# Turns three steps behind the scores, and values four, in the first sixteen steps of three attentions

## The reference

```python
for l in range(DEPTH):                      # DEPTH = 1
    h = _rmsnorm(x, norm_mix[l])
    proj = h @ w_in[l]
    (c_q, c_kv, k_rope, fq, fk, fv, f_logit, cq, ck, cv) = jnp.split(proj, IN_SPLIT_POINTS, axis=-1)
    ya = _mla(c_q, c_kv, k_rope, ...)        # latent: 4 heads, values of 128, all earlier chunks
    yb = _fox(fq, fk, fv, f_logit, ...)      # forgetting: 4 heads of 64, causal, decay in the scores
    yc = _chunk_rel(cq, ck, cv, rel_bias[l]) # chunk: 4 heads of 64, 8 chunks of 64 to the left
    y = jnp.concatenate([_rmsnorm(ya, ga), _rmsnorm(yb, gb), _rmsnorm(yc, gc)], axis=-1)
    x = x + y @ w_o[l]
```

```python
sc = jnp.einsum('bqhd,bkhd->bhqk', qb, k) * scale   # scores, plus a bias or a mask
p = jax.nn.softmax(sc, axis=-1)
out = jnp.einsum('bhqk,bkhd->bqhd', p, v)
```

## Time and profile before

| | |
|---|---|
| median of 3 runs | 2356.68 us (2355.68 to 2357.24) |
| span of the profiled execution, first to last instruction | 2354.8 us |
| PE busy | 2301.3 us (98%) |
| DVE, ACT, POOL busy | 61%, 41%, 37% |
| mean granted TensorE clock | 0.994 |

### The profile page before, as it was taken

One profiled execution on the slowest core, in us unless ns is written; L12 is line 12 of the kernel. 1 busy time (PEld: TensorE's weight loads), 2 busy tenths in 40 slices (PEclk: granted clock), 3 DMA queues, 4 the chain that ended last, 5 costly groups with the idle time before them and its releaser, 6 DMA issues. The chain is left out here.

```text
span 2354.8 us, 30600 instructions
## 1 busy us (share of the span) xinstructions
PE 2301.3 (98%) x11502; PEld 1936.4 (82%) x11502; DVE 1444.1 (61%) x2287; ACT 966.9 (41%) x1963; POOL 872.2 (37%) x737
## 2 busy tenths in 40 slices
PE   6999999999999999999999999999999999999998
PEld 5887878888888888888998887888888888888886
DVE  6999924955354577775634767253495545447776
ACT  4135544532323245455634655134453233234543
POOL 3000125388787800032112121122338878770002
PEclk9999999999999999999999999999999999999999
DMA  5131124233233368664002100144223323336864
GB/s 156 44 71 64 63 83 133 88 119 112 90 116 103 116 242 290 212 209 115 19 19 70 46 5 19 54 143 143 81 72 116 117 85 117 103 122 244 289 214 182
DMA packets 219445, 275.84 MB, mean 117 GB/s; under 512 B 17243, under 2 KB 144956, under 8 KB 216482
## 3 DMA queue, kind: packets, MB, share of 16 engines
q1 hardware_dynamic: 200594, 210.57, 28.7%
q10 hardware_dynamic: 18704, 63.32, 6.9%
HBM read 205.27 MB, written 68.57 MB: 116 GB/s over the span
## 5 line engine op out<-in xcount | busy, mean ns | idle before, releaser
L494 PE MATMUL P<-ah,wh 128*128 128x512 f32 x1120 | 439.3, 392 | 3.2 <-DVE al L524 2.3
L496 PE MATMUL P<-ah,wl 128*128 128x512 f32 x1120 | 436.7, 390 | 0.0
L495 PE MATMUL P<-al,wh 128*128 128x512 f32 x1120 | 436.6, 390 | 0.0
L494 PE MATMUL P<-wh,ah 128*128 128x512 f32 (+2 forms) x1128 | 425.4, 377 | 0.0
L496 PE MATMUL P<-wh,al 128*128 128x512 f32 (+2 forms) x1128 | 423.3, 375 | 0.0
L495 PE MATMUL P<-wl,ah 128*128 128x512 f32 (+2 forms) x1128 | 422.9, 375 | 0.0
L576 POOL TENSOR_TENSOR stats<-stats,epsc 128x1 f32<-128x1 f32 x78 | 31.9, 408 | 794.3 <-ACT xn L1824 420.9
L494 PEld LDWEIGHTS P<-ah,wh 128*128 128x128 f32 x1120 | 210.9, 188 | 47.3 <-DVE al L524 2.5
L496 PEld LDWEIGHTS P<-ah,wl 128*128 128x128 f32 x1120 | 210.8, 188 | 44.1
L495 PEld LDWEIGHTS P<-al,wh 128*128 128x128 f32 x1120 | 210.9, 188 | 43.0
L496 PEld LDWEIGHTS P<-wh,al 128*128 128x128 f32 x1128 | 212.3, 188 | 36.9
(11 more groups left out here) (357 smaller groups left out, 4295.9 us busy)
## 6 DMA issues: line engine op xcount, KB each, us to landing
rf<-ff_rows SPq DMA_DIRECT2D x154, 256.0 KB, 5.3
stage<-in_w_down_dram SPq DMA_DIRECT2D x110, 256.0 KB, 3.7
ff_rows<-sb ACTq DMA_DIRECT2D x22, 1024.0 KB, 5.0
stage<-in_w_gu_dram SPq DMA_DIRECT2D x44, 512.0 KB, 5.1
stage<-in_w_in_dram SPq DMA_DIRECT2D x22, 512.0 KB, 4.0
stage<-in_w_gate_dram SPq DMA_DIRECT2D x22, 512.0 KB, 4.0
stage<-in_w_up_dram SPq DMA_DIRECT2D x22, 512.0 KB, 5.2
ff_rows<-uo ACTq DMA_DIRECT2D x22, 512.0 KB, 3.0
```

Source lines behind the costliest of these rows:

```text
L494: e.matmul(out, lh, rh, start=start, stop=False, skip_group_check=onto)
L495: e.matmul(out, lh, rl, start=False, stop=False, skip_group_check=onto)
L496: return e.matmul(out, ll, rh, start=False, stop=stop, skip_group_check=onto)
```

## The change

In steps 0 to 15 the turns stand three iterations behind the scores and the values four (`lag` is 3 while x < `deep` = 16); from step 16 on it is two and three as before. The two rules meet in iteration 18, where the turns of steps 15 and 16 both fall, and 19, where the values of both fall. For the longer distance there is a fourth buffer of probabilities of 512 columns, in memory that is free then. What hangs on the end of a block (`o`, squares, scaled rows, its turn and its lower half) moves with the values of its last head: for blocks 0 to 3 it comes one iteration later. In forgetting attention the turns of chunk attention's blocks move from iterations 0, 3, 7, ... 27 to 0, 4, 8, ... 28. Sends and filling work keep their iterations. Cross attention keeps the old distances (`deep = 0`). No instruction is added or removed.

```diff
+        deep = 16
...
+        def lag(self, x):
+            return 3 if x < self.deep else 2
+
+        def turned_at(self, it):
+            return [x for x in (it - 3, it - 2) if 0 <= x < self.n and x + self.lag(x) == it]
+
+        def ended_at(self, it):
+            for x in self.turned_at(it - 1):
+                if self.at(x)[1] == self.nh - 1:
+                    return self.at(x)[0]
+            return None
...
+        def prob_free(self, port, x):
+            earlier = [y for y in range(x) if set(self.places(y)) & set(self.places(x))]
+            if earlier:
+                port.wait_ge(*self.last_turn(earlier[-1]))
...
         def pe(self):
-                if 2 <= it <= self.n + 1:
-                    x = it - 2
+                for x in self.turned_at(it):
...
-                if it >= 3:
-                    x = it - 3
+                for x in self.turned_at(it - 1):
...
         def act(self):
-                if 2 <= it <= self.n + 1:
-                    self.copy_turned(AC, it - 2)
+                for x in self.turned_at(it):
+                    self.copy_turned(AC, x)
...
     class Chunked(Heads):
-        probs = [big(f"s2_{i}", [128, 640], 50 + 2.5 * i) for i in range(3)]
+        probs = [big(f"s2_{i}", [128, 640], 50 + 2.5 * i) for i in range(3)] + [
+            sb("s2_3", [128, 512], off["extra"] + 12 * KB)]
...
     class Fox(Heads):
+        narrow_probs = [sb(f"p3n_{i}", [128, 512], off["ah"] + 4 * KB * i) for i in range(3)] + [big("p3n_3", [128, 512], 56)]
...
         def turn_key(self, it):
-            if it >= 9 and it % 4 == 1 and (it - 9) // 4 < NT:
-                return self, (it - 9) // 4
-            if self.kind == "fox" and (it == 0 or it > 0 and it % 4 == 3) and (it + 1) // 4 < NT:
-                return chunked, (it + 1) // 4
+            i = self.ended_at(it - 3)
+            if i is not None:
+                return self, i
+            if self.kind == "fox" and it % 4 == 0 and it // 4 < NT:
+                return chunked, it // 4
...
     class Latent(Fox):
+        narrow_probs = [sb(f"p4n_{i}", [128, 512], off["extra"] + kb * KB) for i, kb in enumerate((0, 4, 8, 2))]
...
-            if it == 3:
+            if it == 4:
                 port.wait_ge(cp, ("mv", 3))
...
     class Cross(Fox):
+        deep = 0
```

More of the change, by code:

```diff
@@ L2960, in act @@
                     W, _, src = self.view(it)
-                    dst = self.probs[it % 3][:, 0:W]
+                    dst = self.prob(it)[:, 0:W]
                     AC.wait_ge(sm, (self.kind, "nm", it))
-                    if it >= 3:
-                        AC.wait_ge(*self.last_turn(it - 3))
+                    self.prob_free(AC, it)
                     e.activation(dst, dst if self.biased else src, ACT.Exp, bias=head_cols(it)[0],
                                  accum_out=head_rows(i)[0][:, h:h + 1]).then_inc(*ex.up((self.kind, it)))
-                if it >= 3 and self.at(it - 3)[1] == self.nh - 1:
-                    self.square(self.at(it - 3)[0])
+                if self.ended_at(it) is not None:
+                    self.square(self.ended_at(it))
                 if it in self.sends:
@@ L2987, in dve @@
             for it in range(self.n + 3):
-                if 2 <= it <= self.n + 1:
-                    self.copy_turned(DV, it - 2)
+                for x in self.turned_at(it):
+                    self.copy_turned(DV, x)
                 self.turned_dve(it - 1)
@@ L3261, in later_dve @@
         def later_dve(self, it):
-            if it >= 7 and it % 4 == 3:
-                i = (it - 7) // 4
+            i = self.ended_at(it - 1)
+            if i is not None:
                 self.scaled(i, yc[:, i, :], gout[:, 768:1024])
@@ L3531, in pt, with places, prob @@
             return self.turned[x % 2][g // 4][:, g % 4:g % 4 + w, :]
+        def places(self, x):
+            return (self.narrow_places[x % 4],) if x < self.deep else ((x % 3, 0), (x % 3, 1))
+        def prob(self, x):
+            return self.narrow_probs[x % 4] if x < self.deep else self.probs[x % 3]
         def width(self, i):
@@ L3623, in later_dve @@
         def later_dve(self, it):
-            if it >= 7 and it % 4 == 3 and (it - 7) // 4 < NT:
-                i = (it - 7) // 4
+            i = self.ended_at(it - 1)
+            if i is not None:
                 self.scaled(i, self.outs[i % 2][:, :], gout[:, self.gain[0]:self.gain[1]])
```

26 lines of the change are left out of this document (15 added, 11 removed).

## The result

The changed kernel takes **2374.79 us** (median of 5 runs, 2374.26 to 2375.81) where the kernel before took 2356.68 on the same chip: a ratio of 1.0074, 95% interval 1.0064 to 1.0085. It is 18.1 us slower; I had said 5.6 us, 2362.3, with a range that ended at 2368. The direction was right, the size was not. The profiled execution spans 2372.5 us, TensorE is busy 2307.9 of them (97%).

A forecast was written before the change was run, and what follows sets the result against it. TensorE, busy 98%, bounds the kernel; only its idle time and slow stretches can change. Chunk +0.3, forgetting +2.8 and latent +2.5 sum to 5.6 us: 2362.3 us against 2356.7, range 2354 to 2368.

The forecast's parts named there:

- What bounds the kernel: Whole kernel: TensorE, busy 98% of 2354.8 us; only its idle time and slow stretches can be won.
- chunk attention's meeting: Iteration 18 of chunk attention: last of nine turns waits for VectorE's copy of step 15, +0.3 us, bounds 0 and 0.7.
- forgetting attention's start: First steps: waits of 1.16 us go, but ScalarE's copy of step 0 comes later; -0.6 us, bounds -1.2 and 0.
- values of step 16 there: Iteration 19 of forgetting attention: values wait bare for VectorE's copy and lower half, +1.2 us, bounds 0 and 2.
- latent attention's meeting: Iteration 18 of latent attention: TensorE waits for VectorE's copy of step 15, behind slow scaled rows; +1.5 us, bounds 0 and 2.5.
- values of step 20: Iteration 23 of forgetting attention: wait for block 3's copy and lower half, partly covered by two turns; +1.0 us, bounds 0 and 2.
- step 16's last turn: Iteration 18 of forgetting attention: waits 1.8 us for ScalarE's copy of step 15; +1.2 us once an old 0.58 us wait goes.
- bounds of 0.5 either way: Start of chunk attention: first exponential comes no earlier, so 0 counted, with 0.5 us either way.
- a rival of 0.20: Clock falls once more in forgetting attention, behind waits of 1.8 and 1.2 us: +2.7 us, 2365.0; chance 0.20.
- middle: Middle of forgetting attention: VectorE sets the pace and the clash with GpSimd stays; 0 us, bounds -2.5 and +1.6.
- It cancels: Rival: waits at 23 and of step 16's last block half hidden; +3.0 us, 2359.7, no change to tell; chance 0.27.
- a clock of 1.00 at 1130 us: Sign in chunk attention that would show the forecast wrong: TensorE's clock staying up there.

The follow-up runs named there:

- mended kernel: Changed kernel with GpSimd waiting for the scaled rows, turns of blocks 2 and 3 one iteration earlier, forgetting attention's send of iteration 17 at 18: 2356.45 us.
- t_oldturn: Changed kernel with the chunk blocks' turns in forgetting attention back at iterations 0, 3, 7, 11, ...: 2374.23 us, ratio 1.0063.
- t_chunk7: Changed kernel with chunk attention's second send at iteration 7, not 6: 2370.80 us, against 2373.37 for the changed kernel.
- d_fox: Lag of three in forgetting attention alone, read against the kernel before: 2366.98 us, ratio 1.0051.
- t_send: Changed kernel with ScalarE's send of iteration 17 in forgetting attention one iteration later: 2372.24 us, against 2373.37 for the changed kernel.
- b_again: The kernel before itself, unedited, executed once more for a second profile: 2354.58 us in one execution.
- b_wait: Kernel before, with GpSimd's lower halves of weights waiting until VectorE's scaled rows of the block just ended are done: 2356.16 us, ratio 1.0000.

## Why the prediction was wrong, step by step

*What bounds the kernel* was right: nothing was to be won but TensorE's idle time and slow stretches, and the copies were not brought forward. The mended kernel shows it, with 4.3 us of waits for ScalarE's copies and the time of before.

*The terms that were waits were nearly all right.* Forecast and measured, in us: chunk attention's meeting 0.3 and 0.35; forgetting attention's start -0.6 and -0.66 (1.16 became 0.20 and 0.30); values of step 16 there 1.2 and 1.18; latent attention's meeting 1.5 and 1.46, its values 1.45 and 1.45, then 1.25 and 1.17. Two were too small: values of step 20, 1.0 and 1.44, so the two turns that I let cover the pair did not; and step 16's last turn, 1.8 and 2.61. There the exponential of step 17 started 3.99 us after its scores, not the 3.06 of the earlier trace rows: the lower half of chunk block 4 had moved in front of its maximum; with that turn back in its old place (t_oldturn) it started 2.55 us after them, and the wait was 1.18. I had counted the moved turns of the attention's own blocks and not those of the chunk blocks.

*The step that failed in chunk attention* was its start, "bounds of 0.5 either way". I looked at the first two waits and at the meeting, and never asked what the scaled rows of block 0 would run beside. The root of block 0 moved by one iteration and the send did not, so GpSimd's half, which had been held back until VectorE was ahead by 0.09 us, now started first, and the scores waited 2.16 us. Measured in place of 0.3: 2.9 us for the stage at like clock, 3.7 as a difference of medians, and 2.6 given back when the send was moved (t_chunk7). The Trainium skill ("SBUF — State Buffer", Who interferes with whom) says that a VectorE instruction with two inputs in SBUF contends with a GpSimd instruction that reads SBUF, that the shared port is an exclusive lock, and that the order of issue decides who is blocked. The trace agrees on both sides: VectorE second takes 2.56 us for 0.48, GpSimd second 2.62 for 2.35. That rule, together with the send's end beside the root's, would have pointed at the clash.

*The step that failed in forgetting attention* was to add waits, put the clock at nothing in the sum and let it be a rival of 0.20. I had put one more fall at 2.7; there were two, of 1.7 us each, behind the waits at 1336 and 1350. The sum from the trace: start -0.7, middle +0.9 (waits of all kinds 4.5 in place of 3.5), step 16's last turn 2.61 less the 0.58 that went, 1.18, 1.44 and 3.4 for the clock make the stage's 8.3 us. d_fox is 10.0 us slower in the median; its profile has 8.4 of them in this stage and 1.5 in latent attention, as slow clock behind the old `mk` wait at 1428 us, so 8.3 is the figure for the stage.

*Latent attention*: 4.0 in the trace in place of 2.5 (4.2 by medians). The meetings were as forecast; the exponential waits are 0.23 and 0.45 in place of 0.3, the copies at the start cost 0.5 more, and TensorE is busy 0.8 us longer, which no row explains.

So the trace's 17.7 us against the 5.6 forecast come apart like this: 5.5 too little for forgetting attention (3.4 of it the clock, 0.8 step 16's last turn, 0.4 step 20, 0.9 the middle), 1.5 for latent attention, 1.0 for chunk attention, and 3.9 ahead of all changed code, which are absent in the third profile of the same kernel and whose cause stays open. At like clock chunk attention's miss is 2.6.

*"It cancels"* was wrong: the waits were bare, and where one was shortened (t_send) the next took up most of it. *One sign was a bad one.* I had called a clock of 1.00 at 1130 us a sign of being wrong. It came in two of the three profiles of the changed kernel, and in b_again without any change, so it tells nothing about the lag. The other signs came as forecast: `al` in 19 and 23, ScalarE's and VectorE's copies in 18, scaled rows of 2.50 us in forgetting attention's block 0 and no wait for `mk`. One did not hold throughout: in latent attention the scaled rows of block 2 took 2.84 us, but those of block 3 took 1.68, not over 2.3.

## What to carry to other kernels

Where a lag changes at one step, one iteration carries two turns and every instruction keyed to a block's end moves by one: list, for each engine, what then stands ahead of the instruction that TensorE waits for, the other stages' instructions included. A buffer is worth only the wait that it brings forward: here it paid in one attention of three, where the moved turn freed VectorE for a copy that the scores needed, and there mostly where the clock fell behind that wait. Waits of TensorE as short as 1.2 us had 1.7 us of slow clock behind them in forgetting attention, and waits of 1.45 us in latent attention had none: put that into the sum, as a chance for each. And compare stages only between profiles whose clock is alike there, or take two profiles of each kernel: a median that moves by what one forecast can be a gain in one stage and a loss to the clock in another, as in t_chunk7 and b_wait.

## What the runs showed of the hardware that I had not expected

A start of 0.07 us against one of 0.09 the other way decided 2.1 us of VectorE's time. It was no toss-up: GpSimd was ahead in all three profiles of the changed kernel and VectorE in both of the kernel before. The clock, however, does not follow from the program alone: the same wait of 1.27 us was followed by 1.2 GHz in one execution of the changed kernel and by 2.4 GHz in another. The Trainium skill ("TensorE: Matmul & The Clock Gate", What's actually happening) says that the check of activity runs free of the kernel's start; these two executions fit that, and no run here shows more of it.
